# Three short 16-bit products behind each group of TensorE in the delta stage, and a ring of six banks

## The chip, the cores and the metric

The kernel runs on one core of one Trainium2 chip. The metric is the device time of the whole program in microseconds (us), the median of several runs.

## The reference

One inference step of a hybrid decoder trunk, for a prompt (16 meta tokens and 512 tokens, one sequence) and for a sample group (8 sequences of 4 tokens) with shared weights:

```
xn   = rmsnorm(h)
proj = xn @ w_in                      # q | k | v | z | a | b for 4 heads of 128, and the 2 x 512 of the convolution group
h    = h + concat[gated_delta_net(...), conformer_conv(...)] @ w_out
h    = h + peer(rmsnorm(h))           # 8 heads, top 16 of 128 x 128 single-neuron experts
y    = rmsnorm(h)
```

The part that matters here is the gated delta rule. For each head and each chunk of C tokens:

```
L      = strict_lower((k * beta) @ k.T) * decay
sol    = solve(I + L, [v * beta | k * beta * exp(G)])      # C x 256
v_new  = sol_v - sol_k @ S
o      = (q * exp(G)) @ S + ((q @ k.T) * decay) @ v_new
S      = S * exp(G_last) + (k * exp(G_last - G)).T @ v_new
```

All results are float32.

## The kernel before

The program is written by hand, engine by engine, with semaphores. It has three large parts: the projections with the convolutions (to about 237 us in the profile), the delta stage (about 237 to 495 us), and then the output projection, the query projection and the experts, where all 128 x 128 experts are computed densely on TensorE (to 2011 us).

**The delta stage.** The prompt is cut into chunks of 128 tokens, tiles 0 to 3, and a chunk of 16, tile 4; tile 5 (`SAMPLE`) is the sample group with 32 rows. A tile is a list of groups. A group is what one call of `each` issues: the same product or transpose for the four heads, into one bank of PSUM, with one increment of TensorE's semaphore on the last (`T.op`). For a tile of 128 rows there are 34 groups, in this order: k, v, gb, khT, kk, kq, ldT, p2, pt2, t1, p4, pt4, t2, p8, t3, n, nt, n2, nt2, nt4, r0a, r0b, r1a, r1b, r2a, r2b, r3a, r3b, wT, ws, qs, o1, su, on. From p2 to nt4 powers of L are multiplied (`prod4`, at line 900 of the profile); r0a to r3b apply them to the right side, two heads at a time (line 958); ws, qs, o1 and su are the products with the state (lines 994, 997, 1000, 1004); k, v, khT, ldT, wT and on are transposes against `ident` (lines 904, 907, 914, 923, 970, 1008). Tile 4 has 23 groups through `each` and the sample tile 17. The sample tile has besides `sw`, four sets of 16 products with 8 columns each (line 980), which do not go through `each`. `ln_tile` issues 15 groups for the layer norm of the convolution part (cs and cn at line 1023, ln at line 1030), not through `each` either.

**Order.** Two tiles are worked side by side. `side_by_side` merges the lists of all tiles by hand-set turns (`FIRST`, `STEP`, `ON_FIRST`), a new tile every 18 turns, and TensorE, VectorE and ScalarE all walk the same merged order. Each engine takes its instructions strictly in that order. VectorE also does the convolution of one channel group as a filler, one step every third turn (line 1555).

**The ring.** Each group writes the bank `RING[i % len(RING)]`, i being its place in the merged order `GROUPS`, and its result is read by VectorE or ScalarE (`e`). Before TensorE writes group i it waits in `free_bank` until the group `len(RING)` places earlier has been read. Bank 3 is for `sw` alone. In the delta stage bank 2 is the seventh of the ring in the kernel before; the banks 0 to 3 are used again by the projections after the stage.

All products of the stage are in float32. The trace shows such a product as two MATMUL records, a transpose as one.

Of the kernel before, what the change touches and what calls it, by code (L numbers as in the profile page):

```python
# [17 lines left out]
BF16 = mybir.dt.bfloat16  # L18
# [4 lines left out]
P = 128  # L23
# [113 lines left out]
def build(nc, ins, outs, counts):  # L137
# [13 lines left out]
    with ctx:  # L151
# [7 lines left out]
        def place(name, shape, dt=F32, region="all"):  # L159
            words = int(np.prod(shape[1:])) * mybir.dt.size(dt) // 4  # L160
            words = -(-words // 8) * 8
            t = at(name, shape, dt, used[region])
            used[region] += words
            assert used[region] <= room
            return t


        ident = place("ident", [P, P])
# [141 lines left out]
        bank = [psum[:, 512 * i:512 * i + 512] for i in range(8)]  # L310
# [80 lines left out]
        def turn(n, ci):  # L391
            if ci >= LN:
                return LN_AT[n][0] + LN_AT[n][1] * (ci - LN), ci
            if n in ON_STEP:
                return ON_FIRST[ci] + ON_STEP[n], ci
            late_ = HEADS - 1 if ci == SAMPLE and not isinstance(n, tuple) and STEP[n] > STEP["sw"] else 0
            return FIRST[ci] + STEP[n] + late_, ci

        def side_by_side(tile, ln_tile, filler=iter(())):
# [14 lines left out]
            for _ in filler:  # L414
# [2 lines left out]
        GROUPS = sorted([(n, ci, e) for ci in range(LN) for n, e in groups(ci) if n != "sw"]  # L417
                        + [(n, LN + t, e) for t in range(NTB) for n, e in (("cs", V), ("cn", V), ("ln", A))],
                        key=lambda x: turn(x[0], x[1]))
        RING = [4, 5, 6, 7, 0, 1, 2]  # L420
        WHERE = {(n, ci): i for i, (n, ci, _) in enumerate(GROUPS)}

        def gbank(n, ci):
            if n[:2] == "su" and n != "su":
                return bank[4 + 2 * (int(n[2]) % 2) + int(n[3])]
            return bank[3 if n == "sw" else RING[WHERE[n, ci] % len(RING)]]

# [27 lines left out]
        def unit_read(eng, u):  # L455

            b = max(b for b in range(nb) if UNIT0[b] <= u)
            (V if BLOCKS[b][0] == "out" else A).wait(eng, "unit", u)
# [310 lines left out]
        def _(pe):  # L769
            mm = pe.matmul  # L770
# [95 lines left out]
            def free_bank(n, ci):  # L866

                i = WHERE.get((n, ci), len(RING))
                if n == "sw":
                    pass  # L870
                elif i >= len(RING):
                    m, cj, e = GROUPS[i - len(RING)]
                    e.wait(pe, m, cj)
                elif i == 0:
                    A.wait(pe, "tails")
                    V.wait(pe, "tails")
                    unit_read(pe, UNIT0[first["out"]] - 1)

            def tile(ci):
                c0, c = CHUNKS[ci]  # L880
                s_ = ci == SAMPLE
# [3 lines left out]
                def group(n, *needs):  # L885

                    free_bank(n, ci)
                    for e, m in needs:
                        e.wait(pe, m, ci)
                    return gbank(n, ci)  # L890

                def each(n, f, width, *needs, only=range(HEADS)):
                    b_ = group(n, *needs)
                    for i, hh in enumerate(only):
                        last = f(b_, i, hh)
                    T.op(last, n, ci)

                def prod4(n, L, R, *needs):

                    each(n, lambda b_, i, hh: mm(b_[0:c, i * c:(i + 1) * c], L[0:c, hh, 0:c], R[0:c, hh, 0:c]),  # L900
                         c, *needs)

                yield "k"
                each("k", lambda b_, i, hh: pe.transpose(b_[0:c, i * P:(i + 1) * P],
                                                         qkvT[:, HEADS + hh, c0:c0 + c], ident[:]), P)
                yield "v"
                each("v", lambda b_, i, hh: pe.transpose(b_[0:c, i * P:(i + 1) * P],
                                                         qkvT[:, 2 * HEADS + hh, c0:c0 + c], ident[:]), P)
                yield "gb"
# [101 lines left out]
            def ln_tile(ci):  # L1011
# [20 lines left out]
                T.op(last, "ln", ci)  # L1032

            side_by_side(tile, ln_tile)
            T.counts["mixer", "last"] = T.n

# [1010 lines left out]
```

## Time and profile before

| | |
|---|---|
| device time, 3 runs | median 2011.06 us (2009.78 to 2013.45) |
| the profiled execution's own time | 2013.25 us |
| its span | 2011.5 us |
| TensorE (PE) busy | 1832.2 us, 91% |
| VectorE (DVE) busy | 1564.5 us, 78% |
| mean granted TensorE clock | 0.949 of full |
| delta stage, 240 to 495.5 us | PE busy 192.15 us, mean granted clock 0.79 |

The profile is of one execution. Times in it are microseconds from the start of the span. "PEclk" is the clock that was granted to TensorE as a share of full speed; over a stretch it is a mean of two levels, 1.0 (2.4 GHz) and 0.5 (1.2 GHz). A row of the timeline merges equal instructions that follow each other; its duration runs from the first start to the last end, and since products are pipelined, the next row begins before it ends. The idle time in square brackets is what the engine waited before the row, and for whom.

### The profile page before, as it was taken

How to read it: one execution, taken by the hardware profiler on the slowest of the kernel's cores; microseconds unless marked ns; L12 is line 12 of the kernel's file. 1: busy time of each engine (PE TensorE's matmuls, PEld its weight loads, DVE VectorE, ACT ScalarE, POOL GpSimd, SP SyncE). 2: the span in 40 equal slices, each digit the busy share in tenths (PEclk: the TensorE clock that was granted, in tenths of full speed). 3: DMA queues.
4: the chain of work that ended last, by engine and by line, in shares of the span. 5: the costliest groups of instructions: out<-in, count | busy, mean ns of one | idle time of the engine just before them, and what ended most of it. 6: DMA issues, size and time to landing. Idle time of an engine off the chain costs nothing.

```text
span 2011.5 us, 29739 instructions
## 1 busy us (share of the span) xinstructions
PE 1832.2 (91%) x11606; PEld 1773.3 (88%) x11606; DVE 1564.5 (78%) x2742; ACT 651.3 (32%) x1029; POOL 937.4 (47%) x676
## 2 busy tenths in 40 slices
PE   3999687777979999999889999998999999999997
PEld 2999676665979999988889999997999999999996
DVE  3596877765348999999899999954688887888854
ACT  3444211122033333322324343432333333333332
POOL 2699899000000057788756656566144343434200
PEclk9999788875979999999999999999999999999998
DMA  6221100000552137877649999999899999999941
GB/s 186 64 83 53 48 1 1 1 1 6 170 160 75 64 131 268 280 255 262 227 157 299 303 300 302 301 308 410 311 349 397 356 359 345 353 359 354 343 172 34
DMA packets 192924, 424.86 MB, mean 211 GB/s; under 512 B 11204, under 2 KB 119264, under 8 KB 184585
## 3 DMA queue, kind: packets, MB, share of 16 engines
q1 hardware_dynamic: 155473, 287.99, 41.5%
q0 software_dynamic: 37312, 134.97, 19.2%
q8 instruction: 92, 1.51, 0.3%
q14 instruction: 47, 0.39, 0.1%
HBM read 361.28 MB, written 62.06 MB: 210 GB/s over the span
## 4 chain that ended last, share of the span: by engine, by line
PE 64%; DVE 26%; issue 3%; DMA 2%; ACT 2%; POOL 2%; DVEq 0%; ACTq 0%; POOLq 0%
PE psum L1137 29%; PE psum L1117 14%; PE psum L816 7%; PE psum L1105 4%; PE psum L811 3%; PE psum L900 2%; DMA rowg<-in_expert_u_rows,idx 2%; DVE sel L1868 1%; PE psum L958 1%; DVE cT L1555 1%; DVE eqa L1865 1%; DVE WR L1482 1%; DVE junk L1890 1%; DVE besti L1817 1%; DVE sring L1821 1%
## 5 line engine op out<-in xcount | busy, mean ns | idle before, releaser
L1117 PE MATMUL psum<-xT,WS 128*128 128x416 f32 x3072 | 607.5, 357 | 22.5 <-POOL WS L754 22.2
L1117 PEld LDWEIGHTS psum<-xT,WS 128*128 128x128 f32 x3072 | 580.0, 191 | 31.6 <-POOL WS L754 26.1
L1137 PE MATMUL psum<-AR,WS 128*128 128x416 f32 x3072 | 578.3, 350 | 2.6 <-DVE AR L1978 2.6
L1137 PEld LDWEIGHTS psum<-AR,WS 128*128 128x128 f32 x3072 | 573.5, 188 | 7.4 <-DVE AR L1978 3.0
L754 POOL TENSOR_TENSOR WS<-RAWP,WS 128x1024 fp32r<-128x1024 f32 x128 | 311.6, 2438 | 506.9 <-ACT WS L1381 505.9
L747 POOL DMA_INDIRECT rowg<-in_expert_v,idx x128 | 182.9, 1429 | 307.9 <-DVE acc L1903 297.9
L816 PE MATMUL psum<-xT,WR 128*128 128x280 f32 (+1 forms) x1968 | 263.7, 297 | 2.5 <-DVE xT L1500 2.5
L816 PEld LDWEIGHTS psum<-xT,WR 128*128 128x128 f32 x1968 | 260.7, 195 | 3.3 <-DVE xT L1500 3.2
L1391 ACT ACTIVATE WS<-RAWP 128x1024 fp32r<-128x1024 f32 x128 | 135.8, 1061 | 351.4 <-PE psum L1137 351.4
L1971 DVE TENSOR_TENSOR WS<-RAWP,WS 128x1024 fp32r<-128x1024 f32 x128 | 156.5, 1223 | 118.8 <-ACT WS L1391 118.8
L1418 ACT ACTIVATE actA<-psum 128x416 f32<-128x416 f32 x128 | 66.3, 518 | 448.4 <-PE psum L1117 417.7
L1890 DVE CUSTOM_DVE_ANT_0 junk<-rowg,psum 128x1024 bf16<-128x1024 f32 x128 | 155.9, 1218 | 56.9 <-DMA rowg<-in_expert_u_rows,idx 55.1
L747 POOL DMA_INDIRECT rowg<-in_expert_u_rows,idx x128 | 164.1, 1282 | 69.7 <-DVE sdot L1890 46.2
L1903 DVE SCALAR_TENSOR_TENSOR acc<-rowg,coef,acc 128x1024 f32<-128x1024 f32 x128 | 163.7, 1279 | 5.4 <-DMA rowg<-in_expert_v,idx 3.0
L737 POOL TENSOR_SCALAR ctmp<-gext,dwcols 128x528 f32<-128x528 f32 x120 | 144.4, 1215 | 5.9
L1381 ACT ACTIVATE WS<-RAWP 128x1024 fp32r<-128x1024 f32 x128 | 134.3, 1051 | 0.0
L741 POOL TENSOR_TENSOR cT<-cT,ctmp 128x528 f32<-128x528 f32 x120 | 114.1, 971 | 5.0
L1953 DVE TENSOR_TENSOR oh<-iotab,pairs 128x1024 bf16<-128x1024 bf16 x52 | 111.5, 2144 | 0.5 <-PE psum L1105 0.5
L1956 DVE TENSOR_TENSOR ohg<-oh,pairs 128x1024 bf16<-128x1024 bf16 x156 | 100.7, 700 | 1.8
L1482 DVE TENSOR_TENSOR WR<-RAW,WR 128x2048 fp32r<-128x2048 f32 (+1 forms) x25 | 57.7, 2308 | 44.1 <-ACT WR L1156 43.9
L900 PE MATMUL psum<-M,M 128*128 128x128 f32 (+2 forms) x504 | 65.5, 282 | 22.4 <-DVE M L1680 15.0
L900 PEld LDWEIGHTS psum<-M,M 128*128 128x128 f32 (+2 forms) x504 | 60.5, 195 | 27.9 <-DVE M L1680 15.7
(324 smaller groups left out, 1960.0 us busy)
## 6 DMA issues: line engine op xcount, KB each, us to landing
RAWP<-in_expert_u SPq DMA_DIRECT2D x64, 1024.0 KB, 6.9
RAWP<-in_expert_v SPq DMA_DIRECT2D x64, 1024.0 KB, 7.8
act_dram<-actA SPq DMA_DIRECT2D x128, 208.0 KB, 3.9
gate_dram<-gblk SPq DMA_DIRECT2D x13, 2048.0 KB, 11.9
Gt<-gate_dram SPq DMA_DIRECT2D x32, 832.0 KB, 7.0
act<-act_dram SPq DMA_DIRECT2D x64, 416.0 KB, 7.9
RAW<-in_w_in SPq DMA_DIRECT2D x8, 1024.0 KB, 6.4
RAW<-in_w_query SPq DMA_DIRECT2D x8, 1024.0 KB, 5.7
```

Source lines behind the costliest of these rows:

```text
L737: G.op(pool.tensor_scalar(t_, x, w, None, ALU.mult))
L747: pool.indirect_dma_start(out=rowg[:, s_ % 4, :], out_offset=None, in_=table, in_offset=bass.IndirectOffsetOnAxis(ap=idx[:, s_ % PAIRS:s_ ...
L754: pool.tensor_tensor(ws(n)[:, 1], raw(n), ws(n)[:, 0].bitcast(F32), ALU.subtract).then_inc(u_low, 1)
L816: last = mm(bank[u % 4][:, 0:hw], W[:, pw, kt, m * P:(m + 1) * P], xT[:, px, kt, half * hw:(half + 1) * hw], **go)
L900: each(n, lambda b_, i, hh: mm(b_[0:c, i * c:(i + 1) * c], L[0:c, hh, 0:c], R[0:c, hh, 0:c]), c, *needs)
L1117: last = mm(bank[e % 2][:, 0:TD], ws(e)[:, pw, kt * P:(kt + 1) * P], xT[:, px, kt, TSP:TPE], start=(kt == 0 and i == 0), stop=(kt == KT - ...
L1137: last = mm(bank[dt][:, 0:TD], ws(NK + e)[:, pw, dt * P:(dt + 1) * P], AR[:, e % 4, pa, :], start=(e == 0 and i == 0), stop=(e == NK - 1 a ...
L1381: act.activation(ws(n)[:, 0], raw(n), ACT.Copy).then_inc(u_high, 1)
L1391: act.activation(ws(n)[:, 0], raw(n), ACT.Copy).then_inc(v_high, 1)
L1890: dve.tensor_tensor_reduce(junk[:, s_ % 2], rowg[:, s_ % 4, :], xnP, 1.0, 0.0, ALU.mult, ALU.add, sdot[:, s_:s_ + 1]).then_inc(dot_done, 1)
L1903: dve.scalar_tensor_tensor(acc[:], rowg[:, s_ % 4, :], coef[:, s_:s_ + 1], acc[:], ALU.mult, ALU.add).then_inc(axpy_done, 1)
L1971: tt(ws(NK + e)[:, 1], raw(NK + e), ws(NK + e)[:, 0].bitcast(F32), ALU.subtract).then_inc(v_low, 1)
```

## The change

Behind each group that `each` issues, after the increment of the semaphore, TensorE now also issues three products of 128 x 128 by 128 x 128 in bfloat16. Both operands are the first 128 16-bit halves of each row of the float32 identity matrix, and the result goes to bank 2, where nothing reads it. Bank 2 leaves the ring, which has six banks then. The groups of `sw` and of `ln_tile` get no such products.

```diff
-        RING = [4, 5, 6, 7, 0, 1, 2]
+        RING = [4, 5, 6, 7, 0, 1]
...
+            def keep_busy():
+
+                for _ in range(3):
+                    mm(bank[2][:, 0:P], ident[:].bitcast(BF16)[:, 0:P], ident[:].bitcast(BF16)[:, 0:P])
+
...
                 def each(n, f, width, *needs, only=range(HEADS)):
                     b_ = group(n, *needs)
                     for i, hh in enumerate(only):
                         last = f(b_, i, hh)
                     T.op(last, n, ci)
+                    keep_busy()
```

## Rows read from the trace of the kernel before

**Rows 1.** The page's busy line and its granted clock in 40 slices.
```profile
PE 1832.2 (91%) x11606; PEld 1773.3 (88%) x11606; DVE 1564.5 (78%) x2742; ACT 651.3 (32%) x1029; POOL 937.4 (47%) x676
...
PEclk9999788875979999999999999999999999999998
```

**Rows 2.** Busy time by stretch in the delta stage, with the granted clock.
```profile
core 0: us, PE busy (x) PEld busy (x) DVE busy (x) ACT busy (x) POOL busy (x), PEclk, DMA share, GB/s
240.00:310.40 70.40, 50.80 (x320) 46.17 (x318) 54.73 (x77) 13.87 (x23) 67.41 (x67) 0.84 0.02 5
310.40:355.60 45.20, 33.45 (x212) 30.82 (x212) 35.15 (x52) 7.01 (x12) 39.56 (x42) 0.88 0.00 1
355.60:396.80 41.20, 32.12 (x212) 29.24 (x212) 30.66 (x53) 7.01 (x12) 0.00 (x0) 0.91 0.00 1
396.80:430.50 33.70, 27.17 (x212) 21.86 (x212) 23.48 (x52) 4.18 (x10) 0.00 (x0) 0.96 0.00 1
430.50:440.10 9.60, 4.66 (x40) 2.67 (x40) 7.23 (x20) 3.46 (x10) 0.00 (x0) 0.50 0.00 1
440.10:463.30 23.20, 22.42 (x149) 20.42 (x150) 4.16 (x11) 4.81 (x19) 0.00 (x0) 0.50 0.00 1
463.30:485.10 21.80, 18.21 (x73) 10.83 (x71) 10.80 (x17) 6.59 (x16) 0.00 (x0) 0.50 0.00 1
```

**Rows 3.** For whom TensorE waits longest, 240 to 495 us.
```profile
PE psum L900 <- DVE M L1680: 15.0, 4, 5.5
PE psum L1008 <- DVE ONB L1734: 9.4, 4, 4.1
PE psum L958 <- DVE RA L1700: 9.3, 4, 3.3
```

**Rows 4.** Timeline of TensorE, the run of groups from r2a of tile 1.
```profile
333.52 1.10 PE L958 MATMUL psum<-RA,M 128*128 128x256 f32 x4 [3.28 <-DVE RA L1700]
...
336.54 1.92 PE L900 MATMUL psum<-M,M 128*128 128x128 f32 x8
338.25 1.09 PE L958 MATMUL psum<-RB,M 128*128 128x256 f32 x4
339.17 1.05 PE L900 MATMUL psum<-M,M 128*128 128x128 f32 x8
...
344.34 1.06 PE L900 MATMUL psum<-M,M 128*128 128x128 f32 x8
```

**Rows 5.** Timeline of VectorE in the same period.
```profile
345.50 0.69 DVE L1676 COPY M<-psum 128x512 f32<-128x512 f32 x1 [0.18 <-PE psum L900]
...
354.92 0.69 DVE L1680 TENSOR_TENSOR M<-M,psum 128x512 f32<-128x512 f32 x1
```

**Rows 6.** Two stretches at half clock, by engine (columns as in rows 2).
```profile
287.20:290.50 3.30, 3.26 (x10) 2.73 (x11) 2.77 (x4) 0.32 (x1) 3.12 (x4) 0.50 0.00 0
...
335.00:338.30 3.30, 3.30 (x14) 2.95 (x13) 3.08 (x5) 0.60 (x1) 3.22 (x4) 0.50 0.00 0
```

**Rows 7.** TensorE's groups by line, 440.1 to 463.3 us.
```profile
L980 PE MATMUL psum<-WQ,SS 128*128 128x8 f32 x64 | 14.2, 360 | 0.3 <-ACT WQ L1156 0.3
L900 PE MATMUL psum<-M,M 16*16 16x16 f32 x56 | 2.6, 185 | 0.0
```

**Rows 8.** Timeline of TensorE in the expert stage: 24 bfloat16 products and what follows, at half and at full clock.
```profile
1029.07 2.74 PE L1105 MATMUL psum<-ohg,oh 128*128 128x128 bf16 x24 [5.36 <-DVE ohg L1956]
1031.57 0.70 PE L1117 MATMUL psum<-xT,WS 128*128 128x416 f32 x1
...
1049.50 1.51 PE L1105 MATMUL psum<-ohg,oh 128*128 128x128 bf16 x24
1050.83 0.43 PE L1117 MATMUL psum<-xT,WS 128*128 128x416 f32 x1
```

**Rows 9.** Weight loads of sw, and the group with the least room in its ring.
```profile
444.93 3.48 PEld L980 LDWEIGHTS psum<-WQ,SS 128*128 128x128 f32 x16 [0.69 <-ACT WQ L1156]
...
426.19 0.68 DVE L1718 TENSOR_TENSOR M<-psum,tok 128x512 f32<-128x512 f32 x1
...
428.14 1.02 PE L958 MATMUL psum<-RA,M 32*32 32x256 f32 x4
```

**Rows 10.** What follows the stage on TensorE.
```profile
501.86 13.22 PE L811 MATMUL psum<-WR,xT 128*128 128x256 f32 x96 [2.51 <-DVE xT L1784]
```

## The prediction

> **What bounds the kernel now.** I read the page first. TensorE is busy 91% of the span and its clock is near full, but for the slices from about 240 to 500 us, where it drops as low as 0.5 [rows 1]. That is the delta stage, the only place the change touches, so I went on with windows over that stage [rows 2]. The reader is to see two different things there. Up to 430 us TensorE is busy 72 to 81% of each period at a mean clock of 0.84 to 0.96, beside a VectorE that is busy nearly as long. From 430.5 to 485.1 us the clock stays at 0.50 throughout, while TensorE is almost never idle from 440.1 to 463.3 us (22.42 of 23.20 us). Then I asked for whom TensorE waits [rows 3]: for t2's result before group n, for r1b's before r2a, four times each. Both are results of VectorE that come late because it works its own list in order. The timelines of one period (tile 1 beside tile 2) show the alternation [rows 4, 5]: after 3.28 us of idle time TensorE runs without a gap from r2a (333.52) to pt4 (344.34), 12 groups; VectorE reads pt4 the moment it is there (345.50, after 0.18 us of waiting for TensorE) and then has work of its own until 355.61, for which TensorE waits. So in each period TensorE sets the time for some 12 us, VectorE for most of the rest.
>
> **The products: how many, and what one costs.** There are 34 groups in each of four tiles, 23 in tile 4 and 17 in the sample tile: 176 groups, 528 products. The nearest row is the expert stage's bfloat16 product of the same shape [rows 8]: 24 of them take 1049.50 to 1050.83, 0.055 us each, at full clock, and 1029.07 to 1031.57, 0.104 us each, at half. Three are 0.17 or 0.31 us. Next comes the group behind them, whose float32 weights have to be loaded while the last short product runs. At half clock 16 such loads take 3.48 us, 0.21 each, so about 0.11 at full clock [rows 9]; a 0.055 us product covers half of that. I add the other half, 0.05 us (0.1 at half clock): 0.22 us a group at full clock, 0.43 at half. The lower bound is 0.17 and 0.31, with the load wholly hidden.
>
> **Which of them are paid.** The semaphore is incremented before the three products, so the readers of a group see nothing of its own three; only the next group does, and only if it would have started at once. Where the next group waits for VectorE anyway, they fall into the idle time and cost nothing. I walked the timeline from 242.41 to 493.28 us and counted the groups whose products delay something on the path:
> - n, n2 and nt2 after the long wait, in each of tiles 0 to 3: each one delays nt, nt2 or k, on which VectorE waits. 3 groups a period; n is at half clock but for tile 0.
> - r2a to ws (r2a, ldT, r2b, p2, r3a, pt2, r3b, t1, wT, p4, ws), all ahead of pt4 in the gapless run [rows 4]: 11 groups in the first three periods, about three of them at half clock; 6 in the fourth, where TensorE has small gaps between them.
> - Others: 7 in the first period (two of k and v, four of p2 to p4, one before kk; five at half clock), 3 in the third, where VectorE's read of gb follows TensorE within 0.1 us.
>
> By period: 13 at full and 8 at half clock; 10 and 4; 13 and 4; 8 and 1. Together 44 at full and 17 at half clock. In the tail, 430.5 to 495 us, all at half clock in the trace: on and pt2 ahead of ln, four between the sets of sw, three among ws, qs and on, three among on, r0a, r0b, and three more at the end: 15. Some are followed by small loads, so I take 0.35 us there.
>
> Cost: 44 x 0.22 = 9.7, 17 x 0.43 = 7.3, 15 x 0.35 = 5.3, together 22.3 us. With the lower prices 44 x 0.17 + 32 x 0.31 = 17.4 us. A bound from below nothing: a product can't make its own group earlier; a gain can only come by the clock.
>
> **What the clock may give back.** In the first four periods the clock fell after idle time, never inside a run; the stretches at 0.5 that then lie in a gapless run cost half of their 3.3 us, some 1.7 us each [rows 6]. p2 at half clock took 1.92 us where the like group takes 1.05 [rows 4]. The long waits before n (5.5 to 3.7 us) stay as they are: the products stand behind the last group and not in the gap, so n and nt stay slow. The waits before r1a and r2a (2.1 to 3.3 us) become shorter by the products of the two or so groups ahead, 0.2 to 0.4 us. A wait of 1.5 us and those of the fourth period, up to 1.36, did not lose the clock. Five falls on the path are thus in doubt, worth 1.5, 1.7, 0.9, 1.7 and 1.7 us, 7.5 in all. I take that 2.5 of them go, 4.2 us, and that some seven paid groups become 0.2 us cheaper with it, 1.5 us. In the tail one or two stretches may come back to full clock, where five groups stand close together (441 to 444 us) and at 462 us; the sets of sw, 14.2 us for 64 records, have three products between them once in 3.5 us and stay slow [rows 7]. I take 2 us of a possible 3.4. Return: 7.7 us, between 0 and 13.4.
>
> A rule of the Trainium skill bears on this (TensorE: Matmul & The Clock Gate, section "Part 4: PE-mode transpose"): a transpose doesn't count as work for the clock as a product does. The stretch 440.1 to 463.3, busy throughout at 0.50, does not contradict it, but most of its time is sw, real products with 8 columns, so the row can't prove it. By the rule alone, real products between the transposes should bring the tail to full clock, which is the second rival below.
>
> **The ring.** With six banks a group waits for the reading of the sixth before it. I compared every group's start with the end of that reading. The least room is r0a of the sample tile: o1 of tile 3 is read to 426.87, r0a starts at 428.14, 1.27 us later [rows 9]; all others have 1.5 us and more. The products make TensorE later and the room larger. Cost: nothing. The cover gone (TensorE earlier by more than 1.3 us there) would cost the difference, under a microsecond.
>
> **After the stage** TensorE's next products wait for VectorE's last pieces [rows 10], and the reload of h, the weights and the experts all follow from there, so a delay passes to the end undiminished.
>
> **The sum.** 22.3 - 7.7 = 14.6 us. On the profiled execution's own 2013.25 us (its span of 2011.5 and 1.75 around it) that is 2027.9 us. The median of the runs lies 2.2 us under that execution, so 2025.7 us for the median.
>
> **Rivals.**
> - *The clock is held (faster).* The products keep TensorE at full clock wherever it has work, in the tail above all. From 440.1 to 485.1 its 40.6 busy us would shrink: sw 14.2 to 7.1, the transposes and 32- and 16-row products by another 10.4. With 13 us for the eight stretches and the four n groups before, and 3.5 us after 494, 34 us come back, against 76 groups x 0.22 = 16.7 us: 17 us faster, 1994 us. It decides from the point where over 17.4 us return, which the periods before the tail can't give. For it: the tail's products have few rows and columns or are transposes, and full 128 x 128 products are something it lacks. Against: sw.
> - *No change.* The three products vanish in idle time, since TensorE idles 63 of 255 us in the stage, and the clock is as before: 2011 us. Against it: the 12 groups without a gap [rows 4].
> - *The ring binds too.* If readers come later than in this trace, four periods with 1 to 2 us of new waiting add some 6 us to the full cost without return: 2011.06 + 22.3 + 6 = 2039 us. Against it: the room above.
>
> **How the numbers follow.** My forecast with its bounds (17.4 - 13.4 = 4 to 22.3 us slower, 2015 to 2034) gets 0.68. The clock held 0.15, no change within 0.2% (4 us) 0.07, the ring or a higher price 0.10. The range leaves out the first rival and the far end of the last: 2009 to 2035 us; the forecast's own is 2015 to 2034. 0.2% is about what a measurement of this kernel can tell from no change. Faster 0.15, same 0.08, slower 0.77.
>
> **What would show it.** In the changed trace: 528 more bfloat16 products, spaced 0.055 or 0.104 us; the run from r2a to pt4 about 2.4 us longer for the same groups at the same clock; n and nt still slow; fewer stretches at 0.5 before r2b; sw still 3.5 us a set; no wait of TensorE for a bank. It is wrong if the tail shows full clock from 440 us on, or if the short products overlap with their neighbours so that a group's start moves by less than 0.17 us.

## The result, and the profile after

The changed kernel took 2019.32 us (median of 12 runs, 2013.93 to 2027.16) against 2012.88 us for the kernel before in the same comparison: a ratio of 1.0039, 95% interval 1.0024 to 1.0055, so 5 to 11 us slower, 8 in the middle. The two medians themselves lie 6.4 us apart, which is inside that interval. The forecast was 14.6 us slower.

The profiled execution of the changed kernel took 2013.93 us, the fastest of its twelve, with a span of 2012.2 us; it must not be set against 2011.5 as if it were the difference. Single executions differ by a few microseconds outside the stage, mostly by where the clock falls. So I measure the stage itself: from the start of k of tile 0 to the start of on of tile 4 it is 242.41 to 493.28 before, 250.9 us, and 238.23 to 500.14 after, 261.9 us: 11 us more. In a second profile of the changed kernel (its repetition below) it is 12 us. The page of the changed kernel counts 12134 products of TensorE (PE). These are the stretches of rows 2 again (same columns, two left out):

```profile
240.00:310.40 70.40, 54.49 (x451) 50.45 (x450) 53.42 (x75) 11.03 (x19) 67.31 (x69) 0.92 0.01 4
310.40:355.60 45.20, 37.55 (x314) 34.52 (x314) 34.04 (x52) 7.01 (x12) 33.01 (x36) 0.94 0.00 1
355.60:396.80 41.20, 34.82 (x312) 32.24 (x311) 30.78 (x52) 7.01 (x12) 0.00 (x0) 1.00 0.01 1
396.80:430.50 33.70, 31.75 (x281) 27.40 (x280) 21.59 (x47) 4.30 (x10) 0.00 (x0) 0.90 0.00 1
...
440.10:463.30 23.20, 22.78 (x171) 20.19 (x170) 5.62 (x14) 4.74 (x19) 0.00 (x0) 0.50 0.01 1
```

Two things are to be read there. There are 12134 - 11606 = 528 more products, as counted. And the clock is higher in the first three stretches (0.92, 0.94, 1.00 against 0.84, 0.88, 0.91 in rows 2), lower in the fourth (0.90 against 0.96) and still 0.50 in the last one shown and up to 485 us. The stretches are fixed in time, so a longer stage puts other groups into them; the table among the experiments goes by groups instead. What a group costs now is plain in the timeline of TensorE, here two groups of tile 0 and the short products (line 882) behind each:

```profile
252.82 1.11 PE L906 MATMUL psum<-M,M 128*128 128x128 f32 x8
253.77 0.33 PE L882 MATMUL psum<-ident 128*128 128x128 bf16 x3
253.93 1.11 PE L906 MATMUL psum<-M,M 128*128 128x128 f32 x8
```

From start to start it is 1.11 us; before, pt2 of tile 2 started at 339.17 [rows 4] and the group behind it at 340.06, 0.89 us apart. That is 0.22 us for three, the forecast price at full clock. Only its place is another: the first short product starts 0.95 us after the group, 0.06 late, and the group behind starts right after the third, 0.16 us on. At half clock, from the start of kk of tile 0 to the start of kq, it is 2.19 us (245.47 to 247.66), against 1.87 before (249.92 to 251.79): 0.32 us for three, where the forecast took 0.43.

Next the first rows, r2a and r2b, of two runs from r2a to pt4: of tile 1 beside tile 2 (from 331.15) and, one period later, of tile 2 beside tile 3 (from 374.14). Below them is VectorE's reading of pt4 at the end of each:

```profile
331.15 1.10 PE L964 MATMUL psum<-RA,M 128*128 128x256 f32 x4 [3.05 <-DVE RA L1706]
...
333.14 2.02 PE L964 MATMUL psum<-RA,M 128*128 128x256 f32 x4
...
374.14 1.10 PE L964 MATMUL psum<-RA,M 128*128 128x256 f32 x4 [1.83 <-DVE RA L1706]
...
375.85 1.08 PE L964 MATMUL psum<-RA,M 128*128 128x256 f32 x4
```

```profile
345.19 0.69 DVE L1682 COPY M<-psum 128x512 f32<-128x512 f32 x1 [0.40 <-PE psum L906]
...
386.55 0.69 DVE L1682 COPY M<-psum 128x512 f32<-128x512 f32 x1 [0.40 <-PE psum L906]
```

The earlier run lost the clock behind its 3.05 us of waiting: r2b took 2.02 us and the run 14.04 (331.15 to 345.19). Before, the same run took 11.98 us, also with one stretch at half clock [rows 4, 5]; so here the change cost 2.1 us and gave nothing back. The later run kept the clock: r2b took 1.08 us and the run 12.41 us. It is 1.6 us shorter than the earlier one, which is what the clock is worth there. Before, the later run took 12.29 us (375.56 to 387.85) and had a stretch at half clock, so there the clock paid for all but 0.1 us of the products.

One more difference is to be seen, in n, the group behind the long wait for VectorE. Of tile 2, before and after:

```profile
355.71 3.52 PE L900 MATMUL psum<-M,M 128*128 128x128 f32 x16 [4.87 <-DVE M L1680]
```

```profile
354.71 1.13 PE L906 MATMUL psum<-M,M 128*128 128x128 f32 x8 [2.77 <-DVE M L1686]
```

Before, n and nt together (x16) took 3.52 us, for the most part at half clock. After, the wait is 2.1 us shorter and n alone (x8) takes 1.13 us, full clock. In tile 3 the wait went from 3.73 to 2.78 us and n took 1.13 us too; in tile 1 it still took 2.05, behind a wait of 4.01.

### The profile page after: what moved, and what is told of

Read it like the earlier page. It is cut to its first block, busy times and chain, and to the rows that moved or that the text cites. A ratio compares the mean times of both kernels' runs of the same rounds, so it can differ in the third digit from the quotient of the medians.

```text
span 2012.2 us, 30796 instructions
## 1 busy us (share of the span) xinstructions
PE 1856.5 (92%) x12134; PEld 1795.2 (89%) x12134; DVE 1565.6 (78%) x2742; ACT 651.3 (32%) x1029; POOL 935.1 (46%) x676
## 4 chain that ended last, share of the span: by engine, by line
PE 65%; DVE 25%; issue 3%; DMA 3%; ACT 2%; POOL 2%; SPq 1%; DVEq 0%; ACTq 0%
PE psum L1143 29%; PE psum L1123 14%; PE psum L816 7%; PE psum L1111 4%; PE psum L811 3%; PE psum L906 2%; DMA rowg<-in_expert_u_rows,idx 2%; DVE sel L1874 1%; PE psum L964 1%; DVE eqa L1871 1%; DVE WR L1488 1%; DVE besti L1823 1%; DVE sring L1827 1%; DVE besti L1835 1%; DVE junk L1896 1%
## 5 line engine op out<-in xcount | busy, mean ns | idle before, releaser
L1111 PE MATMUL psum<-ohg,oh 128*128 128x128 bf16 x1248 | 80.0, 221 | 5.4 <-DVE ohg L1962 5.4
L1111 PEld LDWEIGHTS psum<-ohg,oh 128*128 128x128 bf16 x1248 | 71.0, 99 | 15.4 <-issue 9.7
```

Of the source, the lines that this page charges most:

```text
L1111: last = mm(bank[4 + g % 4][:, k * NK:(k + 1) * NK], oh1[:, b % 2, i, :], ohg[:, b % 2, x, i, :], start=(x == 0), stop=(x == 2))
```

## The experiments

All ratios are to the kernel before, each with its 95% interval; 0.001 is 2.0 us. In the stage lengths, k of tile 0 to on of tile 4, the ends of those two groups are taken: 250.3 us in the kernel before.

The table splits the stage of one profiled execution each at khT of tile 4: the first four periods are from the start of k of tile 0 to there, the tail from there to the start of on of tile 4. Lengths are in us, with the mean granted clock of the part. The kernel before and the ring alone differ by 1.4 and 2.4 us, though nothing waits for a bank; the clock fell at other places. So where the clocks differ, a difference of that size between two executions shows nothing by itself.

| | first four periods | clock | tail | clock |
|---|---|---|---|---|
| kernel before | 190.0 | 0.89 | 60.9 | 0.53 |
| six banks alone | 192.4 | 0.87 | 59.5 | 0.56 |
| the change | 196.4 | 0.94 | 65.5 | 0.53 |
| the change once more | 197.5 | 0.92 | 65.5 | 0.53 |
| six products | 202.1 | 0.97 | 62.0 | 0.72 |
| loads in their place | 201.6 | 0.89 | 67.2 | 0.53 |
| products in the first four periods only | 199.8 | 0.91 | 60.2 | 0.56 |
| products in the tail only | 193.5 | 0.86 | 62.9 | 0.58 |

**Six banks alone.** The short products taken out, the ring left at six.

```diff
-                    keep_busy()
```

> Only the ring of six banks, no short products. My account (the ring costs nothing, the products cost it all): ratio to the kernel before 1.000, within 2 us, and TensorE waits for a bank nowhere. Rival (the ring binds): 3 us or more slower, with new idle time of TensorE that ends at a group's reading six places earlier, as the changed kernel shows it once, at khT of tile 4.

0.9993 (0.9983 to 1.0002). Stage 251.4 us. No group waits for its bank: the least room between the reading six places earlier and a group's start is 1.27 us, at r0a of the sample tile, the group named in the forecast. The wait at khT of tile 4 that the expectation speaks of, 1.73 us in the changed kernel, is for the group's own operand KH, which VectorE writes (line 1652), and not for a bank. The ring of six costs nothing that can be measured.

**The change once more, and twice the products.**

```diff
-                for _ in range(3):
+                for _ in range(6):
```

> The changed kernel once more, as the yardstick of this call: 6 to 10 us slower than the kernel before, if the measured 1.0039 is the size. In a second trace the stage from k of tile 0 to on of tile 4 should again take about 11 us more than the 251.5 us of the kernel before.

> Six short products behind each group instead of three. My account (a price of 0.055 us for each on the path, about 0.22 for three, with the clock giving back a part): three more add 0.165 us on some 76 groups, 12.5 us, less 2 to 4 us of clock that come back besides; 16 to 20 us slower than before in all. Rival (mostly hidden, the measured loss being something else): less than 12 us slower. Rival (the clock decides): if six keep the tail at full clock, 440 to 485 us, the time falls under that of three.

Three products: 1.0048 (1.0036 to 1.0060), 7 to 12 us slower; stage 262.4 us. Six: 1.0050 (1.0035 to 1.0065), 10 us slower. My 16 to 20 us failed. Six stand where the second account put them, under 12 us, but not for its reason, since they are not hidden: the first four periods are some 5 us longer than with three. The tail is 3.5 us shorter in return. Its mean clock is 0.72 instead of 0.53, and sw runs at its full speed in part.

```profile
455.46 1.95 PE L986 MATMUL psum<-WQ,SS 128*128 128x8 f32 x16
```

This is the first set of sw, 1.95 us instead of the 3.5 that it took before; the second took 2.58 us. The stage is 263.6 us long all the same, against 262.4 with three: the clock that came back about paid for the products added.

**The same TensorE time without the columns.** One float32 product of 8 columns, with its two weight loads, in place of the three.

```diff
-                for _ in range(3):
-                    mm(bank[2][:, 0:P], ident[:].bitcast(BF16)[:, 0:P], ident[:].bitcast(BF16)[:, 0:P])
+                mm(bank[2][:, 0:8], ident[:], ident[:, 0:8])
```

> Instead of three bfloat16 products of 128 columns one float32 product of 8 columns, with two weight loads: about the same TensorE time a group (0.21 us at full clock, 0.43 at half), with 16 columns of data instead of 384. If the short products give back some of their cost through the clock, this one does not and is 12 to 20 us slower than before, with as many stretches at half clock as before. If the clock plays no part in the result, it costs the same 6 to 10 us as the change.

1.0076 (1.0062 to 1.0091), 15.3 us slower, in the expected range and clear of the change's 1.0048. Groups in an unbroken run start 1.09 to 1.11 us apart, as with the three products, and the mean clock is that of the kernel before, 0.89 and 0.53 in the table:

```profile
368.83 1.11 PE L963 MATMUL psum<-RA,M 128*128 128x256 f32 x4
369.78 0.28 PE L881 MATMUL psum<-ident 128*128 128x8 f32 x2
369.92 1.14 PE L915 MATMUL psum<-tri,tok 128*128 128x128 f32 x8
```

So the price on the path with hardly any return is about 15.3 us, 5.6 more than the change cost in the same comparison (9.7 us, 0.0048 x 2012). Not all of the 5.6 is clock, because the two prices are alike only in the first four periods. Behind the small groups of the tail, at half clock, the load costs 0.45 us and the three products 0.29 (from start to start of such groups 0.77 and 0.61 us, and 0.32 without). The table shows the same: the tail with loads is 1.7 us longer at the same clock of 0.53. So of the 5.6 us some 4 came back by the clock, an estimate, and all of it ahead of the tail. In the first four periods the change is 4.2 to 5.2 us shorter than the loads, at 0.92 to 0.94 instead of 0.89, and a third execution with the same products there (below) 1.8 us shorter, at 0.91. The stage is 268.3 us in this trace, 17 more than in that of the ring alone.

**By part.** The products only ahead of khT of tile 4 (the first four periods, the diff), or only from there on (the tail, with `>=`).

```diff
-                    keep_busy()
+                    if WHERE[n, ci] < WHERE["khT", 4]:
+                        keep_busy()
```

> The three products only behind the groups ahead of khT of tile 4, so in the first four periods. By my working these cost 9.7 + 7.3 = 17 us and get 5.7 us back: 11 us slower. In the changed kernel's trace the clock came back more often there; if that holds over many runs, 2 to 6 us slower. Rival (all of the loss sits in the tail): no change.

> The three products only behind khT of tile 4 and the groups that follow. By my working 5.3 us and 2 us back: 3 us slower; in the changed kernel's trace no clock came back in the tail, so 4 to 6 us slower. With the run before it should add up to the whole change. Rival (the products belong there): faster.

First four periods: 1.0020 (1.0006 to 1.0034), 4.0 us slower, far from the 11 of my working and inside the second figure. Tail: 1.0013 (0.9998 to 1.0027), 2.6 us slower, with an interval that just reaches 1. In the table these two kernels are 7.4 and 3.4 us longer in their part than the ring alone, so the parts differ between executions too. My lower figure for the tail was 3 us, the higher 4 to 6; the interval doesn't tell them apart. Together they are 6.6 us, beside the whole change's 7.9 and 9.7.

**Products in the idle time only.** None behind every group; instead blocks behind eleven groups that stand ahead of idle time. The longest (65 products behind t3 of tile 1) fills most of it, others a part.

```diff
+            FILL = {("khT", 0): 20, ("khT", 1): 15, ("kq", 1): 12, ("t3", 1): 65, ("khT", 2): 15, ("kq", 2): 26,
+                    ("t3", 2): 55, ("khT", 3): 8, ("kq", 3): 14, ("t3", 3): 33, ("r0a", SAMPLE): 25}
...
-                    keep_busy()
+                    keep_busy(FILL.get((n, ci), 0))
```

> No product behind every group; 8 to 65 short products at eleven places only, behind the groups after which TensorE has nothing to do for 1.5 to 5.5 us (t3, kq, khT of several tiles, r0a of the sample tile), so that they fill the idle time. If idle time is what loses the clock and the price of the products on the path is what made the change slower, this one has the return without the price: mean clock 0.98 or more from 250 to 430 us, n and nt at 1.1 us each, 6 to 12 us faster than before. Rival (the clock isn't worth anything, VectorE sets these periods): no change. Rival (the fillings overrun): slower.

> The kernel that filled eleven idle times, once more and on the same chip as the next two, since its first result (ratio 0.9967) is near the noise: 0.995 to 0.9985 again if the return by the clock is real; 1.000 if it was chance.

0.9967 (0.9950 to 0.9985), and in a second comparison 0.9978 (0.9965 to 0.9992): 4.4 to 6.6 us faster than the kernel before, 12 or more faster than the change. It beats both kernels. The expected mean clock of 0.98 was not reached: in the second one's trace it is 0.83, 0.92, 0.97 and 0.94 in the stretches of rows 2. Its block behind khT of tile 0 ran at full clock (20 products in 1.28 us), but 3.70 us of waiting for ScalarE came behind it, and from 247 to 255 us the clock was 0.50. The stages of the two profiled executions are 250.5 and 250.6 us long, no shorter than before. So the gain is in the medians of 21 runs, and which periods carry it isn't shown by these two traces. Two other traces with nearly the same blocks have shorter first four periods: 186.9 us at a mean clock of 0.94 with the longer fillings below, and 185.9 us at 0.95 with the fillings of the last experiment, against 190.0 before and 192.4 with the ring alone.

**The same fillings made of loads.** A float32 product of 8 columns for every four short ones.

```diff
-                for _ in range(times):
-                    mm(bank[2][:, 0:P], ident[:].bitcast(BF16)[:, 0:P], ident[:].bitcast(BF16)[:, 0:P])
+                for _ in range((times + 2) // 4):
+                    mm(bank[2][:, 0:8], ident[:], ident[:, 0:8])
```

> The same eleven fillings of about the same length, made of float32 products of 8 columns with their weight loads (one for four short products). If it is data columns that hold the clock, and not TensorE being occupied, this one loses the clock as the kernel before does and is no faster: ratio 0.999 to 1.003. If occupation is enough, it is as fast as the filling with short products.

1.0009 (0.9997 to 1.0022): no gain, and clear of the 0.9978 of the short products in the same comparison. Its first four periods are 192.5 us long, at a clock of 0.87. The place ahead of n of tile 1 shows why. First the filling with short products, then the one with loads:

```profile
304.25 3.79 PE L882 MATMUL psum<-ident 128*128 128x128 bf16 x65
309.16 2.02 PE L909 MATMUL psum<-M,M 128*128 128x128 f32 x16 [1.11 <-DVE M L1689]
```

```profile
301.72 4.29 PE L882 MATMUL psum<-ident 128*128 128x8 f32 x32
307.40 3.75 PE L909 MATMUL psum<-M,M 128*128 128x128 f32 x16 [1.38 <-DVE M L1689]
```

In both TensorE was busy up to 1.1 to 1.4 us ahead of n. Behind the short products n and nt took 2.02 us, full clock, behind the loads 3.75, as in the kernel before. So a block that kept TensorE as long occupied did not keep the clock. The two blocks differ in the number format, in the columns and in the share of weight loads at once; which of these counts isn't shown.

**Three products ahead of idle time only, and longer fillings.**

```diff
+                    if n in ("khT", "kq", "t3") or (n, ci) == ("r0a", SAMPLE):
+                        keep_busy()
```

```diff
+            FILL = {("khT", 1): 15, ("kq", 1): 20, ("t3", 1): 75, ("khT", 2): 15, ("kq", 2): 34,
+                    ("t3", 2): 65, ("khT", 3): 10, ("kq", 3): 24, ("t3", 3): 45, ("r0a", SAMPLE): 35}
```

> Three short products behind khT, kq and t3 of each tile and r0a of the sample tile only, the groups that mostly stand ahead of idle time: 18 of the 176 groups. The price on the path should be near nothing, and the idle times become 0.2 us shorter each. If the price of the products on the path made the change slower, this is no slower than the kernel before: 0 to 3 us faster. If the loss came from somewhere else (the ring, a switch between number formats, the longer program), it is still slower by a few us.

> The fillings without the one behind khT of tile 0, which ran at half clock and delayed kk there by some 2 us in its profile, and with 75, 65 and 45 products behind t3, 20, 34 and 24 behind kq and 35 behind r0a of the sample tile. If the fillings still end before the data come, 2 to 4 us faster than the first filling, 8 to 10 us faster than before. Rival (they overrun, as at half clock each takes 0.104 us): no better than the first filling.

The first: 0.9990 (0.9979 to 1.0001), 2 us faster or nothing. It has the short products, the switch of formats and the ring of the change, and no loss: the loss belongs to the products on the path. The second (tuned): 0.9987 (0.9974 to 1.0000), 2.6 us faster; longer fillings did not add to the gain. In its profile the stage is 247.2 us, the shortest of all, with the clock at 0.89, 0.92, 1.00 and 0.99 in the stretches of rows 2, and yet its median is above that of the first filling. The intervals of the two overlap, so no difference between them is shown. The expectation, 8 to 10 us faster than before, failed. Its premise, a block at half clock that delayed kk, isn't what the profiles of the first filling show.

**Fillings, and products throughout the tail.** Four behind each group of the tail, four behind each cn, three behind each product of sw but the last of a set.

```diff
+                    late_ = WHERE[n, ci] >= WHERE["khT", 4]
+                    keep_busy(FILL.get((n, ci), 4 if late_ else 0))
...
+                            if q < NSEQ - 1:
+                                keep_busy(3)
...
+                    keep_busy(4 if n == "cn" else 0)
```

> As the run before, and in the tail four products behind each group of each kind and three behind each product of sw but the last of a set. If real products between transposes and loads lift the clock there, it is at full from about 440 us on, a set of sw takes 1.8 + 1.2 = 3 us instead of 3.5, a transposing group 0.66 instead of 0.87, and the time is another 5 to 10 us under the run before. If the clock stays at half there, the 28 products in a set of sw alone cost 2.2 to 2.9 us each, and it is 12 us or more slower than the run before.

1.0026 (1.0009 to 1.0043), 10 to 12 us slower than the filling alone. The loss is in the tail: from khT of tile 4 to on it is 73.3 us long, against 59.4 with the filling alone. The clock stayed at half through all of sw, while TensorE was never idle:

```profile
445.00:468.00 23.00, 23.00 (x188) 22.58 (x185) 1.17 (x4) 1.66 (x5) 0.00 (x0) 0.50 0.01 1
```

A set of sw then takes 5.2 us instead of 3.5. With six products behind the groups, in the run further up, the clock was full from 450 to 455 us and through the first set of sw. What decides it there these runs do not tell.

## Why the forecast came out as it did

**The side and the mechanism were right.** The products are paid where TensorE is not idle, the clock gives back less than they cost, and the ring costs nothing. The time fell inside the range, though below the forecast's middle: 8 us (5 to 11), and 10 us in the second comparison, against 14.6.

**The split between the parts was not right.** The working gives 17.0 - 5.7 = 11.3 us for the first four periods and 5.3 - 2 = 3.3 us for the tail. In the first four periods the three traces with these products show 4.0, 5.1 and 7.4 us against the ring alone, and the runs with products only there 4.0 (1 to 7): too dear in all. In the tail both traces of the change show 6.0 us, that of the products there alone 3.4, and its runs 2.6 with an interval up to 5.4. So in the two executions of the change the errors have opposite signs, and its sum came nearer than its parts by luck; whether the tail is too cheap over many runs isn't shown. Of the 29 groups of the tail that have products, 15 were counted as paid; 6.0 us at 0.29 each would be some 20, an estimate.

**The price of three products: right at full clock, too high at half.** From start to start it is 0.22 us at full clock, as forecast, and 0.32 at half, where 0.43 was taken: the 0.1 us for the next group's weights did not show.

**"Which of them are paid": over-sized, the term that was off.** The 22.3 us stand against 15.3 us measured with the loads, which have the same price at full clock and little return; the forecast's lower price would have given 17.4 us. The stage of that trace against that of the ring alone shows where. In the first four periods it is 9.2 us longer, where 44 x 0.22 + 17 x 0.43 = 17.0 was forecast; with 0.32 at half clock it would have been 15.1. In the tail it is 7.7 us longer, where 5.3 was forecast, since there the loads take 0.45 us and not 0.35. The largest part is in the second period, from the end of n of tile 1 to the end of n of tile 2: 45.3 us with the loads and 45.3 without, where 10 x 0.22 + 4 x 0.43 = 3.9 was counted. Two things that returned time there are seen. A VectorE instruction that takes 1.67 us beside GpSimd's convolution in the kernel before falls behind the end of that convolution once the stage is later against it, and takes 0.69 us (below): 1.0 us. And n of tile 2 took 1.13 us with the loads instead of some 2.05, because the clock hadn't fallen behind the wait, which is 2.81 us there and 4.80 without the loads: 0.9 us. For the other 2 us I have no row, and they stay open.

**The return of the clock: 7.7 forecast, some 4 estimated from the runs.** Of the 7.7, 5.7 were put in the first four periods. Its place was right only in part. The groups behind the waits before r1a and r2a did mostly keep the clock, as forecast. But the forecast held that the long waits before n stay as they are and n stays slow. They went from 5.51, 4.87 and 3.73 us to 4.01, 2.77 and 2.78, and n of tiles 2 and 3 took 1.13 us in the change's trace; in the second one only n of tile 3 did. In the tail, where 2 of the 7.7 were put, the change's trace shows none: sets of sw still take 3.45 to 3.53 us each, and the clock is 0.50 from 440 to 485 us.

```profile
448.46 3.52 PE L986 MATMUL psum<-WQ,SS 128*128 128x8 f32 x16
...
452.52 3.53 PE L986 MATMUL psum<-WQ,SS 128*128 128x8 f32 x16
```

Three steps of that working don't hold as written. 2.5 of falls worth 7.5 us in five are 3.75 us, not 4.2. The upper bound of 13.4 us has no working that leads to it: 7.5 + 1.5 + 3.4 is 12.4. And the clock did not always fall before a run: at 335.0 us [rows 6] it fell 1.5 us inside the run that began at 333.52.

**The rivals.** The clock held throughout (the first in the list, which the text on transposes calls the second): false for three products. For six it was held in a part of the tail, and even then about paid for itself. No change: false, and the run with products ahead of idle time only shows what it took for it to be true. The ring: false.

**The rule named in the forecast,** that transposes don't count for the clock, wasn't put to the test by itself. In the Trainium skill the page TensorE: Matmul & The Clock Gate, section "Why this matters for your kernels", advises against idle gaps between bursts of matmuls. The fillings with short products agree (0.9967 and 0.9978); the filling with loads, at 1.0009, shows that here not every instruction in such a gap did.

## What to carry to other kernels

Products that are to hold TensorE's clock belong into its idle time: behind the groups of an unbroken run they cost their full time, here 0.22 us for three, and together more than the clock returned. It matters what fills the gap: here 128-column bfloat16 products kept the clock for the next group, and a block of 8-column float32 products, as long and mostly weight loads, did not. Before counting on the return, price the kernel with equally long instructions that bring none; but compare the two prices at both clock levels first, since here they agreed in the first four periods and not in the tail. And check a forecast by parts: a sum can come out better than its parts.

## What was unexpected

**VectorE beside GpSimd.** In the kernel before, the instruction at line 1720, both of whose inputs are in SBUF (the same tensor twice, a square), took 1.67 us at 350.00 while GpSimd's convolution was running (it ends at 351.8), and so did its fellow in the trace of the six banks (the first row below); in the run with loads (the second) it came at 353.35, behind the end of the convolution at 349.3:

```profile
349.98 1.68 DVE L1721 TENSOR_TENSOR M<-qkvT 128x512 f32<-128x512 f32 x1
```

```profile
353.35 0.69 DVE L1725 TENSOR_TENSOR M<-qkvT 128x512 f32<-128x512 f32 x1
```

Other VectorE instructions next to it, which read PSUM, took 0.69 us in either. In the Trainium skill the page GPSIMD Engine Reference, section "1. Specifications", names contention with VectorE instructions that have two inputs in SBUF; these rows agree. Not every such row does: in the kernel before, the instruction ahead of it (line 1719, 349.27 to 349.96, also two inputs in SBUF) took 0.69 us, though a row of GpSimd had begun at 349.39. So a delay elsewhere can be partly paid back because it moves VectorE's work out from beside GpSimd.

**Six products cost no more than three** (1.0050 and 1.0048). Only with six was the clock higher in the tail, 0.72 in place of 0.53 by the table. And a stretch that is busy throughout with a mixture of short products and 8-column products stayed at 0.50 for 23 us.
